# Norm sums by matmuls with ones, and another order around pooling and the first head, in a pooling and differential attention trunk

## The reference

```python
def _rmsnorm(x, g):
    return x * rsqrt(mean(x * x, axis=-1) + 1e-6) * g

x = x + _pool_mixer(_rmsnorm(x, norm_mix[0]), pool_w[0], pool_scale[0])   # windows 2, 4, 8, 16
x = x + _mlp(_rmsnorm(x, norm_mlp[0]), w_mlp_in[0], w_mlp_out[0])
kv = _rmsnorm(x, kv_norm) @ w_kv
k = _rmsnorm(kv[..., :1024].reshape(b, s, 8, 2, 64), k_norm)
v = kv[..., 1024:].reshape(b, s, 8, 128)
q = _rmsnorm((h @ w_q).reshape(b, s, 8, 2, 64), q_norm) * 64 ** -0.5      # h = _rmsnorm(x, norm_mix[1])
p = softmax(q k^T + rel_bias[bucket(i - j)], masked to j <= i)             # for both halves
o = (p[half 0] - lam * p[half 1]) @ v                                      # per head
x = x + (_rmsnorm(o, subln) * (1 - lambda_init)) @ w_o
x = x + _mlp(_rmsnorm(x, norm_mlp[1]), w_mlp_in[1], w_mlp_out[1])
```

## Time and profile before

| | |
|---|---|
| median of three executions | 969.94 us |
| the profiled execution | 970.49 us |
| its span, first to last instruction | 968.70 us |
| PE busy | 954.0 us (98%) |
| DVE busy | 681.1 us (70%) |
| ACT busy | 464.6 us (48%) |
| POOL busy | 82.3 us (8%) |
| mean granted clock of PE | 0.998 |

### The profile page before, as it was taken

How to read it: one execution, slowest core, us unless ns; L and a number is a source line. 1 busy time by engine, 2 the same in 40 slices (tenths; PEclk the granted TensorE clock), 3 DMA queues, 4 the chain that set the end, 5 groups by cost and what they waited for, 6 DMA issues and landing times.

```text
span 968.7 us, 13034 instructions
## 1 busy us (share of the span) xinstructions
PE 954.0 (98%) x5143; PEld 813.1 (84%) x5143; DVE 681.1 (70%) x959; ACT 464.6 (48%) x588; POOL 82.3 (8%) x66
## 2 busy tenths in 40 slices
PE   8999999999999999999999999999999999999998
PEld 7788998998898898778888887888888888888877
DVE  4976766666676678877777777667767676677685
ACT  7644334334333437576666765345433433433432
POOL 1201000000000000122222220000000000010010
PEclk9999999999999999999999999999999999999999
DMA  6427682385457534143232222334676269238534
GB/s 228 138 84 232 131 260 87 88 228 163 118 113 205 160 59 130 44 115 86 72 86 84 78 74 93 109 102 113 191 200 191 90 125 261 89 87 225 165 98 120
DMA packets 99212, 128.94 MB, mean 133 GB/s; under 512 B 3201, under 2 KB 61618, under 8 KB 99162
## 3 DMA queue, kind: packets, MB, share of 16 engines
q1 hardware_dynamic: 85178, 98.33, 30.8%
q0 software_dynamic: 13984, 29.91, 16.8%
HBM read 126.11 MB, written 4.74 MB: 135 GB/s over the span
## 4 chain that ended last, share of the span: by engine, by line
PE 85%; DVE 7%; ACT 4%; issue 3%; DMA 1%; SPq 0%; DVEq 0%; ACTq 0%
PE bank L1375 27%; PE bank L1377 26%; PE bank L1376 26%; PE bank L1565 2%; DVE w_low L918 2%; PE bank L1575 2%; DVE kq_sum_buf L1175 1%; ACT w_high L655 1%; PE bank L1519 1%; DMA work<-in_x_dram 1%; ACT h_high_buf L613 1%; ACT w_high L607 0%; DVE work L1273 0%; ACT a_high_buf L812 0%; DVE a_low_buf L1244 0%
## 5 line engine op out<-in xcount | busy, mean ns | idle before, releaser
L1375 PE MATMUL bank<-h_high_buf,w_high 128*128 128x512 f32 x640 | 252.5, 394 | 0.7 <-DVE h_low_buf L927 0.4
L1377 PE MATMUL bank<-h_high_buf,w_low 128*128 128x512 f32 x640 | 249.4, 390 | 0.0
L1376 PE MATMUL bank<-h_low_buf,w_high 128*128 128x512 f32 x640 | 249.2, 389 | 0.0
L918 DVE TENSOR_TENSOR w_low<-raw,w_high 128x2048 fp32r<-128x2048 f32 (+1 forms) x68 | 147.3, 2166 | 66.8 <-ACT w_high L655 49.1
L1375 PE MATMUL bank<-a_high_buf,w_high 128*128 128x256 f32 (+1 forms) x592 | 184.4, 312 | 2.2 <-DVE a_low_buf L927 1.4
L1377 PE MATMUL bank<-a_high_buf,w_low 128*128 128x256 f32 (+1 forms) x592 | 183.0, 309 | 0.0
L1376 PE MATMUL bank<-a_low_buf,w_high 128*128 128x256 f32 (+1 forms) x592 | 182.8, 309 | 0.0
L1375 PEld LDWEIGHTS bank<-h_high_buf,w_high 128*128 128x128 f32 x640 | 120.2, 188 | 28.7 <-issue 2.2
L1377 PEld LDWEIGHTS bank<-h_high_buf,w_low 128*128 128x128 f32 x640 | 120.1, 188 | 25.4
L1376 PEld LDWEIGHTS bank<-h_low_buf,w_high 128*128 128x128 f32 x640 | 120.3, 188 | 23.6
L664 ACT ACTIVATE work<-work 128x512 f32<-128x512 f32 x64 | 40.1, 632 | 181.3 <-DVE work L971 181.2
(11 more groups left out here) (152 smaller groups left out, 1171.1 us busy)
## 6 DMA issues: line engine op xcount, KB each, us to landing
raw<-in_w_mlp_out_dram SPq DMA_DIRECT2D x24, 1024.0 KB, 6.2
raw<-in_w_mlp_out_dram POOLq DMA_DIRECT2D x24, 1024.0 KB, 8.7
raw<-in_w_mlp_in_dram SPq DMA_DIRECT2D x16, 1024.0 KB, 5.5
work<-in_w_mlp_out_dram SPq DMA_DIRECT2D x8, 1024.0 KB, 4.7
work<-in_w_mlp_in_dram SPq DMA_DIRECT2D x8, 1024.0 KB, 6.7
raw<-in_w_kv_dram SPq DMA_DIRECT2D x16, 512.0 KB, 4.0
xT<-in_w_mlp_out_dram SPq DMA_DIRECT2D x8, 1024.0 KB, 4.7
xT<-in_w_mlp_in_dram SPq DMA_DIRECT2D x8, 1024.0 KB, 7.0
```

The costliest lines, as they stand in the source:

```text
L918: dve.tensor_tensor(w_low_buf[s][:, 0:cols], src[:, 0:cols], f32(w_high_buf[s][:, 0:cols]), ALU.subtract)\
L1375: pe.matmul(acc, w_hi, m_hi, start=start, stop=False, skip_group_check=onto)
L1376: pe.matmul(acc, w_hi, m_lo, start=False, stop=False, skip_group_check=onto)
L1377: return pe.matmul(acc, w_lo, m_hi, start=False, stop=stop, skip_group_check=onto)
```

## The change

**Sums by ones.** ACT squares K, Q and the head's result straight from the bank in which they were made. PE sums over channels and turns in one: the squares (128 channels x 128 tokens) are the weights, and two columns of ones the moving side; for K and Q `half_ones` has a one for the channels of its half only. The turns of the raw data and the reductions on DVE are gone. DVE adds epsilon from the bank, in halves of eight values; K's root, inverse and spread come apart from Q's.

**Order in a head.** K's sums stand in the middle of Q's projection, K's turn behind it, Q's sums behind the probabilities. ACT splits the K half of the next weights once K's projection is done. Heads 1 to 5 are a loop; head 6 is written out, with the first two chunks of the output projection's input. The first head's K, Q and V projections are cut and ordered anew, and V's low part is split right after the last add of the MLP.

**Start.** The bands are loaded after the parameters. DVE squares the last x tile by a custom instruction. One root over all four tiles replaces two. The zero matmul is gone: each matmul of a band starts its own columns. Mixes and pooling products alternate by groups, and the pooling weights are split in halves. The dots for lambda come after the pooling, their exp after K's and Q's roots.

```diff
-            def split_high_first(u, landed_count):
+            def split_high_first(n, landed_count):
+
                 act.wait_ge(w_landed[1], landed_count)
+                act.wait_ge(k_proj, n)
+                act.activation(w_high_buf[1][:, 0:UNIT // 2], raw[1][:, 0:UNIT // 2], ACT.Copy).then_inc(half_high, 1)
+
+            def split_high_rest(u):
                 act.wait_ge(w_used, u - 1)
-                act.activation(w_high_buf[1][:, 0:UNIT // 2], raw[1][:, 0:UNIT // 2], ACT.Copy).then_inc(half_high, 1)
-
-            def split_high_rest():
                 act.activation(w_high_buf[1][:, UNIT // 2:], raw[1][:, UNIT // 2:], ACT.Copy).then_inc(w_high, 1)
...
             act.activation(tok_root[:, 0:1], eps[:, :], ACT.Sqrt).then_inc(tok_sq, 1)
-            for i in range(TT):
+            for i in range(TT - 1):
                 act.wait_ge(x_landed[i], 16)
                 act.activation(h_tok[:, i, :], x_tok[:, i, :], ACT.Square, accum_out=tok_ss[:, i:i + 1]).then_inc(tok_sq, 1)
-                if i >= TT - 2:
-                    tiles = slice(0, TT - 1) if i == TT - 2 else slice(TT - 1, TT)
-                    act.wait_ge(tok_sq, i + 2)
-                    act.activation(tok_root[:, tiles], tok_ss[:, tiles], ACT.Sqrt, scale=1.0 / D, bias=eps[:, 0:1]).then_inc(tok_rooted, 1)
+            act.wait_ge(tok_sq, TT)
+            act.wait_ge(tok_last_sq, 1)
+            act.activation(tok_root[:, :], tok_ss[:, :], ACT.Sqrt, scale=1.0 / D, bias=eps[:, 0:1]).then_inc(tok_rooted, 1)
...
-                    act.wait_ge(params_turned, 1)
-                    act.activation(params[:, :], I[0][:, 0:N_PARAM], ACT.Copy).then_inc(params_ready, 1)
-                act.activation(xT[:, c, :], bank[c][:, :], ACT.Copy).then_inc(xt_copied, 1)
-
+            act.wait_ge(tok_inverse, 1)
+            act.activation(h_tok[:, TT - 1, :], x_tok[:, TT - 1, :], ACT.Copy, scale=tok_rstd[:, TT - 1:TT]).then_inc(h_tok_last, 1)
+            copy_xt(4)
+            act.wait_ge(params_turned, 1)
+            act.activation(params[:, :], I[0][:, 0:N_PARAM], ACT.Copy).then_inc(params_ready, 1)
+            for c in ACT_CHUNKS[1:4]:
+                copy_xt(c)
+            act.wait_ge(w_landed[0], 16)
+            act.activation(w_high_buf[0][:, 0:UNIT // 2], raw[0][:, 0:UNIT // 2], ACT.Copy).then_inc(pool_half_high, 1)
...
+            def square_k(n):
+
+                act.wait_ge(k_proj, n + 1)
+                act.activation(ksq, I[0][:, :], ACT.Square).then_inc(kq_sq, 1)
...
+            def head(h, first, last=False):
+                n = h + 1
                 exps(h)
+                bring_table(ACT.Sqrt)
                 if not first:
-                    o_squares(h - 1, I[3])
-                copy_k(h + 1)
-                split_v(h + 1)
-                bring_table(ACT.Sqrt)
-                copy_q(h + 1)
-                split_high_first(U_HEAD + 4 + 2 * h, kq_landed(h + 2))
-                at_highs(h)
-                project(h + 1)
-                kq_roots(h + 1)
+                    square_k(n)
+                    copy_k(n)
+                split_v(n)
+                if last:
+                    o_high(0)
+                    o_high(1)
+                k_root(n)
+                split_high_first(n + 1, kq_landed(n + 1))
+                square_q(n)
+                copy_q(n)
+                k_high(n)
+                at_highs(h, range(1))
+                q_root(n)
                 if not first:
-                    o_roots(h - 1)
+                    o_roots(h - 1, I[3])
+                at_highs(h, range(1, 3))
                 bring_table(ACT.Exp)
-                kq_highs(h + 1)
-                split_high_rest()
+                q_high(n)
+                split_high_rest(U_HEAD + 2 + 2 * n)
...
                 take_4(l, q, 1)
+                if l == 0 and q == NQ - 1:
+                    split_low(U_HEAD + 1, 0, 1024)
 
...
             dve.memset(bias_rows[0:H, S:REL], MASKED).then_inc(bias_rows_ready, 1)
+            dve.wait_ge(x_landed[TT - 1], 16)
+            dve.tensor_tensor_reduce(out=h_tok[:, TT - 1, :], in0=x_tok[:, TT - 1, :], in1=x_tok[:, TT - 1, :], scale=1.0, scalar=0.0,
+                                     op0=ALU.mult, op1=ALU.add, accum_out=tok_ss[:, TT - 1:TT]).then_inc(tok_last_sq, 1)
             dve.wait_ge(tok_rooted, 1)
-            dve.reciprocal(tok_rstd[:, 0:TT - 1], tok_root[:, 0:TT - 1]).then_inc(tok_inverse, 1)
+            dve.reciprocal(tok_rstd[:, :], tok_root[:, :]).then_inc(tok_inverse, 1)
...
+            def add_k_eps(n, b):
+
+                dve.wait_ge(k_summed, n + 1)
+                dve.tensor_tensor(kq_sum_buf[:, 0:8], b[:, 0:8], kq_eps[:, 0:8], ALU.add).then_inc(k_total, 1)
...
+            def k_inverses(n):
+                dve.wait_ge(k_rooted, n + 1)
+                dve.reciprocal(kq_rstd_buf[:, 0:8], kq_root_buf[:, 0:8]).then_inc(k_inverse, 1)
+                dve.wait_ge(k_inverse, n + 1)
+                spread(ksq, kq_rstd_buf[:, 0:8]).then_inc(k_spread, 1)
...
                 combine(h, 3)
-                split_low(U_HEAD + 3 + 2 * h, 0, 1024)
-                if not first:
-                    o_sums(h - 1)
-                at_lows(h)
-                kq_sums(h + 1)
-                kq_inverses(h + 1)
+                split_low(U_HEAD + 1 + 2 * n, 0, 1024)
+                if last:
+                    o_low(0)
+                    o_low(1)
+                add_k_eps(n, I[0])
+                k_inverses(n)
+                k_norm(n, I[0])
+                add_q_eps(n, I[1])
+                at_lows(h, range(1))
+                q_inverses(n)
                 if not first:
                     o_inverses(h - 1)
-                kq_norms(h + 1)
+                at_lows(h, range(1, 3))
+                k_low(n)
+                q_norm(n, I[1])
                 if not first:
                     o_norm(h - 1, O[3])
-                kq_lows(h + 1)
-                take_v(h + 1)
+                q_low(n)
...
+            def mix(c):
                 if c >= 4:
-                    pe.wait_ge(h_low, c - 3)
+                    pe.wait_ge(mixed_low, c - 3)
                 else:
                     pe.wait_ge(xt_copied, c + 1)
 
-                pe.matmul(I[c % 4][:, :], a_high_buf[:, 0, 0:P], a_high_buf[:, 0, :], start=True, stop=False)
                 for i in range(TT):
                     n = min(BAND, S - i * P)
+                    if c == 0:
+                        if i < TT - 1:
+                            pe.wait_ge(h_tok_ready, i + 1)
+                        else:
+                            pe.wait_ge(h_tok_last, 1)
                     last = pe.matmul(I[c % 4][:, i * P:i * P + n], h_tok[:, i, c * P:(c + 1) * P],
-                                     band_sb[:, min(i, 1), c // (KC // G), 0:n], start=False, stop=i == TT - 1)
+                                     band_sb[:, min(i, 1), c // (KC // G), 0:n],
+                                     start=i == 0, stop=True, skip_group_check=i > 0)
...
+            def column_sums(b, src, ones):
+                for i in range(TT):
+                    last = pe.matmul(b[:, 2 * i:2 * i + 2], src[:, i * P:(i + 1) * P], ones[:, :], start=True, stop=True)
+                return last
+
+            def k_sums(n, b):
+
+                pe.wait_ge(kq_sq, 2 * n + 1)
+                pe.wait_ge(kf_ready, n + 1)
+                column_sums(b, ksq, half_ones).then_inc(k_summed, 1)
...
+            project(U_HEAD, 1, 0, I[0], h_high_buf, h_low_buf, None, range(0, 4), ready=H_K, order=KV_ORDER)
             pe.wait_ge(w_low, U_HEAD + 2)
-            project(U_HEAD + 1, 0, 0, I[2], h_high_buf, h_low_buf, None, range(0, 3))
+            project(U_HEAD + 1, 0, 0, I[2], h_high_buf, h_low_buf, None, range(0, 3), order=KV_ORDER)
+            project(U_HEAD, 1, 0, I[0], h_high_buf, h_low_buf, k_proj, range(4, KC), ready=H_K, order=KV_ORDER)
             project(U_HEAD, 1, 1024, I[1], a_high_buf, a_low_buf, None, range(0, 6), ready=H_Q)
-            turn(kf, I[0], kf_ready, 0, kq_raw_turned)
+            project(U_HEAD + 1, 0, 0, I[2], h_high_buf, h_low_buf, None, range(3, 5), order=KV_ORDER)
             project(U_HEAD, 1, 1024, I[1], a_high_buf, a_low_buf, w_used, range(6, KC), ready=H_Q)
-            project(U_HEAD + 1, 0, 0, I[2], h_high_buf, h_low_buf, None, range(3, 6))
-            turn(qf, I[1], qf_ready, 0, kq_raw_turned)
-            project(U_HEAD + 1, 0, 0, I[2], h_high_buf, h_low_buf, w_used, range(6, KC))
+            k_sums(0, O[0])
+            project(U_HEAD + 1, 0, 0, I[2], h_high_buf, h_low_buf, None, range(5, 6), order=KV_ORDER)
+            q_sums(0, O[1])
+            project(U_HEAD + 1, 0, 0, I[2], h_high_buf, h_low_buf, w_used, range(6, KC), order=KV_ORDER)
             norm_stats(NORM_KV)
             pe.wait_ge(half_low, 1)
-            pe.wait_ge(kq_sq, 1)
-            project(None, 1, 0, I[0], h_high_buf, h_low_buf, None, range(0, 4))
```

(17 more changed lines are left out.)

382 lines of the change are left out of this document (216 added, 166 removed).

## The result

The changed kernel takes 977.06 us (median of six runs, 975.35 to 979.96), the kernel before 969.95 (six runs, 968.29 to 970.57): 1.0078 times as long, 95% interval 1.0058 to 1.0099. That is slower by 7.1 us; 978.5 was forecast. The profiled execution took 979.96 us, 9.5 more than the profiled one of before, with a span of 978.2. Runs at a far lower mean clock (one of the experiment k_later, 1061 us at 0.847, and two of the kernel before, 1581 us at 0.556) are left out of every median and range in this document.

A forecast was written before the change was run, and what follows sets the result against it. TensorE (PE) was taken as the bound, busy 954.0 of 968.7 us. Terms 6.8 + 1.9 + 1.7 + 0.5 - 1.4 - 0.9 = +8.6 us gave 979.1 against the profiled execution, forecast as 978.5; range 971.5 to 982.5.

The forecast's parts named there:

- the signs it named: L1656 groups of eight 112 ns apart, heads of 26.6 us, first-head wait before K's turn with low clock, mix from about 13.2.
- heads 1 to 6: Loop heads: three swaps less an old wait give +1.13 us a head, 6.8 for six; bounds 6.0 to 9.0.
- first head without the clock: First head: swaps +1.4, new wait before K's turn +3.6, old waits -2.9, V's turn -0.2; +1.9 us, bounds -1.5 to +3.
- clock behind its wait: After the first head's wait: clock falls for 3.5 us, half of it lost, +1.7 us; bounds 0 and 3.5.
- MLP to first head: Between MLP and first head: two swaps add 0.9, old idle goes in part; +0.5 us, bounds -1.0 and +1.5.
- pooling and mix: Start: zero matmuls -1.7, low clock -0.4, pooled x wait -0.3, later mix +1.0; -1.4 us, bounds -2.8 and +1.
- last head: Last head: sum adds 0.46, the 1.12 us wait ahead of the output projection's second half goes; -0.9 us, bounds -1.3 and 0.
- the swap of a turn for a sum: On PE: sum 0.91 us for turn 0.44, so 0.46 to 0.47 each; 24 times 11.1 us if nothing else moved.
- The open price: Start: is the first custom instruction dear (4.59 us before), or stalled behind POOL? Took the second; otherwise start 4.4 us later.
- rival 1: Further DVE stall: dear first custom instruction, +4.4 us (983), or K's spread behind POOL's subtraction in six heads (985); chance 0.14.
- (2): Whole kernel: no new wait and all old waits go, offsetting the swaps' 11.1 us; 969.1, the same; chance 0.10.
- (3): All 24 sums: one pass, four instructions, 0.44 us like a turn; 967.4, faster; chance 0.08 including (2) going further.

The follow-up runs named there:

- k_later: Changed kernel, but in head 0 ScalarE also splits the K half of the next weights ahead of K's root; 981.11 us.
- one_pass: Changed kernel with the 24 sums by ones as fp32r instead of fp32, four instructions a sum instead of eight; 969.78 us, ratio 1.0009.
- b_o_ones: Kernel before, with only the squares of a head's result summed by ones on TensorE; K, Q and all orders untouched; 970.72 us, ratio 1.0017.
- k_first_dve: Changed kernel, but in head 0 VectorE does K's epsilon, inverse and spread ahead of splitting V's low part; 974.46 us.
- b_no_zero: Kernel before, without the matmul of zeros ahead of each mix; 969.29 us, ratio 0.9997.
- zero_back: Changed kernel with the matmul of zeros put back ahead of each of the eight mixes; 980.71 us, ratio 1.0115.
- old_start: Changed kernel with ScalarE's squares and two roots for the token tiles as before, no custom square; 977.55 us, ratio 1.0077.
- joined_v: Changed kernel with fp32r sums, the output projection's first inputs made as before, and V's weights for head 1 split before head 0; 964.75 us, ratio 0.9948.
- joined_pool: Changed kernel with fp32r sums and V's weights for head 1 split before head 0, the low part by GpSimd instead of VectorE; 965.84 us, ratio 0.9968.

## Why the prediction was right

The direction, the mechanism and the time (978.5 against 977.06, inside 971.5 to 982.5) came out. So did the signs it named: groups of eight at L1656 (some 0.10 us apart, not 0.112), heads of 26.44 us (not 26.6), a wait before K's turn of the first head with low clock behind it in the profile, and a mix from 13.13 us. Term by term, against the profiles:

| term | forecast | profiles | shown by |
|---|---|---|---|
| heads 1 to 6 | +6.8 | +5.6 | one_pass, b_o_ones |
| first head without the clock | +1.9 | +1.7 | k_first_dve |
| clock behind its wait | +1.7 | 4.3 (others 0 to 4.3 by their mean clock) | k_first_dve, k_later |
| MLP to first head | +0.5 | +0.3 | the stages only |
| pooling and mix | -1.4 | -1.6 | b_no_zero, zero_back, old_start |
| last head | -0.9 | -0.9 | b_o_ones in part (-0.5) |

**Heads 1 to 6.** The mis-sized term is the swap of a turn for a sum, 0.46. Within a row of transposes a turn takes 0.44 and a sum 0.81 between starts, so 0.37; the 0.10 on the product behind comes once per group of small matmuls, not once per swap. A head has one such group more than before (K's sums stand alone), so 3 x 0.37 + 0.10 - 0.25 for the wait that went is 0.96, against 0.94 measured. What the earlier trace rows showed were single groups, and I counted their edge three times.

**First head.** K's turn was forecast at 416.0 with PE there at 412.3, it came at 414.16 with PE there at 411.0: all of it 1.3 to 1.8 us early, mostly because the head began 1.2 us earlier (401.49 against 402.65). The wait of 3.6 was 3.0 to 3.2, for the reason given.

**The clock.** That it falls behind this wait was right, its size was not: I took one value, half of the 3.5 us of the earlier trace rows, and the bound of 3.5 was too low. In the profiled run 9.0 us ran at 0.50. But runs differ, from no loss to 4.3 us, and the median run lost 1.6 (977.06 less the 975.5 of the runs at 0.998). That the one value fits the median is luck. The Trainium skill (TensorE: Matmul & The Clock Gate, What's actually happening) says of a kernel's start that the number of matmuls at the low level differs from run to run of the same kernel. Carried over to a wait in the middle, which that passage does not do, it gives a spread of prices; the runs here have one, with 4.4 us between equal programs at 0.998 and 0.993.

**Pooling.** The sum -1.4 came out by terms of which two did not: the later mix (+1.0) and the low clock's share (-0.4) lie off the path (old_start). The 1.7 for the matmuls of zeros held, but it is paid back in full only in the new order by groups (zero_back 1.9, b_no_zero 0.5 to 0.7). The new order and start with the zeros kept are worth nothing: zero_back's MLP begins at 36.55, before's at 36.25, and that 0.3 stood in no term. The weak step is the one from 1.18 and 0.97 us a mix to 1.7 for eight: I priced PE's row and did not ask what PE would wait for next, which in the order of before was DVE's low part of the mix (0.88 us in b_no_zero).

**The open price.** The custom square took 1.23 us at its first use (1.24 was forecast), so that part of rival 1 falls, and the reading of the earlier trace rows, that DVE had stood behind POOL, holds: in b_no_zero the first one is slow again, 4.05 us, and again ends 0.1 us behind a GpSimd subtraction, and joined_v and joined_pool show the same stall on other operations. The Trainium skill (SBUF — State Buffer, Who interferes with whom) lists copies among the operations that can take the port pair shared with GpSimd. By that rule the stall of joined_pool was to be expected, and the trace agrees, 2.39 us for 0.43.

**Rivals.** (1) A stall of DVE in the heads did not come: PE has no idle time in six heads. (2) "No new wait" is false, but its other half, that the old waits in the heads go, is true. (3) A sum in one pass was false of the change as it is (eight instructions) and true of one_pass, which came to 969.8, the 967.4 of that rival and 2.4 more, with waits of its own in head 0 and in the last head.
